# Banded attention: GpSimd adds each key tile's weights in one operation of 1024 columns instead of two of 512

## What is computed

```python
WINDOW = 128
s_ctx = jnp.einsum('bnqhgd,bchd->bnhgqc', qb, kc).astype(jnp.float32) * GQA_SCALE
s_band = jnp.einsum('bnqhgd,bnkhd->bnhgqk', qb, kb).astype(jnp.float32) * GQA_SCALE
valid = (jnp.abs(qpos - kpos) <= WINDOW) & (kpos >= 0) & (kpos < n)
s_band = jnp.where(valid[None, :, None, None], s_band, -jnp.inf)
p = jax.nn.softmax(jnp.concatenate([s_ctx, s_band, s_sink], axis=-1), axis=-1).astype(v.dtype)
o = (jnp.einsum('bnhgqc,bchd->bnqhgd', p[..., :nc], vc)
     + jnp.einsum('bnhgqk,bnkhd->bnqhgd', p[..., nc:nc + 3 * BLOCK], vb))
```

## Time and profile before

| | |
|---|---|
| median of 3 runs | 2767.04 us (2765.52 to 2770.16) |
| profiled execution: time, span | 2770.5 us, 2768.7 us |
| PE busy | 2566.3 us, 93% |
| PEld busy | 1979.2 us, 71% |
| DVE busy | 1419.2 us, 51% |
| ACT busy | 1153.6 us, 42% |
| POOL busy | 381.1 us, 14% |

### The profile page before, as it was taken

One profiled execution on the slowest core, in us unless ns is written; L12 is line 12 of the kernel. 1 busy time (PEld: TensorE's weight loads), 2 busy tenths in 40 slices (PEclk: granted clock), 3 DMA queues, 4 the chain that ended last, 5 costly groups with the idle time before them and its releaser, 6 DMA issues. The chain is left out here.

```text
span 2768.7 us, 38552 instructions
## 1 busy us (share of the span) xinstructions
PE 2566.3 (93%) x14759; PEld 1979.2 (71%) x14759; DVE 1419.2 (51%) x2283; ACT 1153.6 (42%) x1977; POOL 381.1 (14%) x415
## 2 busy tenths in 40 slices
PE   4999998999999999989999999899998999999787
PEld 3778987877778878933337778786334877798776
DVE  5113265666655514666764723411777547265752
ACT  6112344454454321134443622311767647333662
POOL 1000020010020000046761000000000010004710
PEclk8999999999999999989999999999999999998889
DMA  7430010000112131110002220102000220111012
GB/s 257 174 139 24 18 33 1 1 1 1 62 54 91 47 61 46 32 37 1 1 1 91 92 78 30 59 3 76 1 1 24 84 88 31 38 47 62 1 54 76
DMA packets 87991, 139.73 MB, mean 50 GB/s; under 512 B 19513, under 2 KB 54738, under 8 KB 87682
## 3 DMA queue, kind: packets, MB, share of 16 engines
q1 hardware_dynamic: 70592, 75.90, 8.8%
q0 software_dynamic: 16976, 61.30, 6.2%
q10 hardware_dynamic: 242, 0.07, 0.0%
HBM read 120.47 MB, written 16.78 MB: 50 GB/s over the span
## 5 line engine op out<-in xcount | busy, mean ns | idle before, releaser
L169 ACT ACTIVATE WORK<-PS 128x512 f32<-128x512 f32 (+5 forms) x309 | 152.6, 494 | 659.2 <-PE PS L863 388.7
L863 PE MATMUL PS<-HT_R,W_R 128*128 128x512 f32 (+1 forms) x896 | 334.3, 373 | 0.0
L862 PE MATMUL PS<-WORK_R,W_R 128*128 128x512 f32 (+1 forms) x736 | 271.4, 369 | 0.0
L861 PE MATMUL PS<-WORK_R,W_R 128*128 128x512 f32 (+1 forms) x672 | 250.0, 372 | 14.4 <-DVE W_R L169 9.9
L169 ACT ACTIVATE HT<-PS 128x1024 f32<-128x1024 f32 (+6 forms) x211 | 156.0, 739 | 161.0 <-PE PS L1296 126.4
L989 PE MATMUL PS<-WORK_R,HT_R 128*128 128x512 f32 x528 | 210.3, 398 | 8.8 <-DVE W_R L169 7.5
L863 PE MATMUL PS<-W_R,WORK_R 128*128 128x256 f32 (+3 forms) x704 | 215.2, 306 | 0.0
L990 PE MATMUL PS<-WORK_R,MIXT_R 128*128 128x512 f32 x544 | 214.1, 394 | 0.0
L991 PE MATMUL PS<-W_R,HT_R 128*128 128x512 f32 x528 | 207.4, 393 | 0.0
L862 PE MATMUL PS<-W_R,HT_R 128*128 128x256 f32 (+2 forms) x688 | 206.2, 300 | 0.0
L926 PE MATMUL PS<-BASE,WORK 128*128 128x128 f32 (+1 forms) x1186 | 175.2, 283 | 25.3 <-DVE WORK L169 16.8
(11 more groups left out here) (328 smaller groups left out, 5587.3 us busy)
## 6 DMA issues: line engine op xcount, KB each, us to landing
MIXT<-in_w_mod POOLq DMA_DIRECT2D x8, 2048.0 KB, 8.7
x_scratch<-WORK POOLq DMA_DIRECT2D x24, 512.0 KB, 2.9
WORK<-x_scratch POOLq DMA_DIRECT2D x24, 512.0 KB, 3.6
W<-in_odd_w_in SPq DMA_DIRECT2D x12, 1024.0 KB, 5.2
W<-in_even_w_in SPq DMA_DIRECT2D x5, 2048.0 KB, 7.9
W<-in_w_mod SPq DMA_DIRECT2D x4, 2048.0 KB, 20.8
WORK<-in_x POOLq DMA_DIRECT2D x16, 512.0 KB, 8.7
W<-in_e_w_in SPq DMA_DIRECT2D x6, 1024.0 KB, 5.9
```

The source lines that it names most:

```text
L169: self.last = Signalled(self, issue(*args, **kwargs))
L861: mm(out, a[0], b_[0], start=k == 0, stop=False)
L862: mm(out, a[1], b_[0], start=False, stop=False)
L863: return mm(out, a[0], b_[1], start=False, stop=k == KT - 1)
```

## The change

The loop over the two halves goes; one operation adds all 1024 columns of a step. The buffers, the waits around a step and the step's one increment of `summed` stay. There are 60 such sums (76 steps less the 16 with k = 0), so that 120 operations become 60. No other engine's instructions change, neither in number nor in order.

```diff
@@ -3261,10 +3261,7 @@
                         if k == 1 and m >= 2:
                             pool.wait_ge(totalled, m - 1)
                         total = psum_of(m)
-                        was = halves8(GPT[(n - 1) % 3]) if k == 1 else total
-                        for par in range(2):
-                            added = add_up(total[:, par, :], was[:, par, :], halves8(GPT[n % 3])[:, par, :], ALU.add)
-                        added.then_inc(summed, 1)
+                        add_up(total, halves8(GPT[(n - 1) % 3]) if k == 1 else total, halves8(GPT[n % 3]), ALU.add).then_inc(summed, 1)
                         if k == 2 and done < 2 * KT and m >= 4:
```

## The result

The changed kernel takes 2782.02 us (median of 6 runs, 2777.11 to 2783.96); the kernel before, run beside it, 2768.48 (6 runs, 2765.52 to 2774.22). The ratio is 1.0044, with an interval of 1.003 to 1.0058: slower, by less than half a per cent. The profiled execution took 2778.17 us with a span of 2776.3, which is 7.6 more than the span of before.

What follows compares the result with a forecast made beforehand. PE bounds the kernel, through its waits for DVE, which POOL's operations hold. Terms 6.5 + 0.9 + 2.8 - 0.7 + 2.9 = 12.4 us take the profiled execution from 2770.5 to 2782.9; median 3.5 below, so 2779.5, range 2773.5 to 2785.

Steps and rivals of the forecast that it cites:

- PE's four waits of two groups: Ahead of PE's fifth top (L1324) and transpose (L1348), odd and even groups; DVE ends each; 1.93 us more in all.
- The merged sum: POOL's sum of 1024 columns takes 2.37 us, bounds 2.30 and 2.45, instead of 2.62 for a pair.
- The odd group's fifth top: At L1324, the whole sum holds DVE's low parts, so PE starts 1.09 us later.
- Its transpose: Odd group's transpose (L1348): DVE waits for a whole sum, but the last 8 columns find POOL idle; adds 0.
- The even group: Low parts ahead of the fifth top +0.13 us; SCALAR_TENSOR_TENSOR ahead of the transpose waits for a whole sum, +0.71.
- The stage: Banded attention: odd fifth tops 6.5, even ones 0.9, even transposes 2.8, first groups -0.7, end +2.9; sum 12.4 us.
- the term there: Group 13 and the last two groups: operations such as the diagonal's wait for a whole sum, estimated +2.9 us in all.
- The clock: Rival, 7%: longer PE waits in the last groups bring one or two more lower-clock stretches, 2 to 5 us more.
- ended inside a sum: Rival, 7%: the 1024-column sum lets DVE in halfway, say at 1.2 us; -4.5 us, 2762.5.
- the tie at the SCALAR_TENSOR_TENSOR: At both transposes POOL's sum comes 0.10 us first; rival, 7%: DVE passes first, +5.5 us, 2772 to 2773.
- 24 places in twelve groups: Range: four places per two groups follow the sum's length one to one; 2.30 takes 1.7 us off, 2.45 adds 1.9.
- The hold: A DVE operation with inputs in SBUF and a POOL operation exclude each other; whoever comes first keeps the place.

Runs made afterwards that it cites:

- The two part kernels: Against the kernel before, only each group's first sum (k = 1) merged, or only the others (k > 1), the rest kept as halves: 1.0036 and 1.0016.
- The fill kernel: Against the changed kernel, POOL fills the 1024 columns with 1.0 instead of each merged sum, reading nothing; softmax's denominator left out: 2750.7 us, one run.
- shorter pieces: Each sum as four operations of 256 columns instead of one of 1024, in the old order: 0.9982 against the kernel before.
- quarters: Sums as four operations of 256 columns, first sum behind the low parts, slab subtractions behind a group's last sum: 0.9948 against the kernel before.
- halves and merged sums with both moves: First sum waits for the low parts, slab subtractions move from k = 2 to k = 4; two 512-column sums or one of 1024: 0.9976 and 0.9964 against before.

## Why the prediction was right

*The place.* PE's four waits of two groups set the stage's pace. The 33.2 to 33.3 us that remain in all twelve rows of the table bear this out.

*The merged sum.* 2.37 us taken from the 1280-column row; 58 of the 60 take 2.34 to 2.40, the other two were held themselves.

*The odd group's fifth top.* Forecast +1.09, measured +1.11 (gap 0.11 to 1.22). Its low parts take 2.25 us where I had said 2.2.

*Its transpose.* Forecast 0, measured -0.05. The reason given was right as well: a whole sum held the SCALAR_TENSOR_TENSOR, and the last 8 columns found POOL idle (0.17). The two part kernels show that the zero belongs to both parts together: each alone shortens this wait, by 0.88 and 0.54.

*The even group.* Forecast +0.13 and +0.71, measured +0.13 and +0.67. Two groups: +1.85, forecast +1.93.

*The stage.* From the first fifth top to the last, +9.4 us, where the terms gave 6.5 + 0.9 + 2.8 - 0.7 = 9.5. Ahead of the first nothing changed (-0.1). Behind the last fifth top it is +4.3, and the term there was +2.9. PE's waits there grew by 2.8 (0.68 at the transpose of group 13, 0.10 at the top of 1432.12, 1.10 ahead of the L1373 of 1449.97 and 0.95 at the transpose of 1455.61), so the term was right as a sum, though its parts, "1.09 each, with some slack", weren't worked out one by one. **The other 1.5 us are the clock, which the sum had at nothing.** In all +13.65 instead of +12.4.

*The clock.* It was one rival, at 2 to 5 us for one or two stretches more at the lower level. No stretch was added, but the one behind the stage's last long wait became 6.8 us long instead of 3.4, for 1.5 us. The other rivals fell: none of DVE's two-input operations ended inside a sum; the tie at the SCALAR_TENSOR_TENSOR went to POOL by 0.10 to 0.13 us; the waits reached PE.

*What was wrong in the working.* "24 places in twelve groups" that follow the sum's length is too many. By the prediction's own terms an odd group's transpose adds 0 whatever the length, so 17 places do (6 + 7 + 4): the bounds are then 1.2 down and 1.4 up, not 1.7 and 1.9, a sum of 2.25 us would take 2 us off the total and not 3, and a hold would have to be given up earlier than after 1.9 us to eat the 12.4. The hold was also put too widely, as one of any DVE operation with its inputs in SBUF. A one-input reduce in SBUF isn't held: in after the one below runs while POOL's second slab subtraction does (from 1360.08 to 1361.36). This changes no term of the sum.

```profile
1360.23 0.18 DVE L169 TENSOR_REDUCE SMX<-HT 128x8 f32<-128x24 f32 x1
```

*The measurement.* 2782.0 against 2779.5 forecast. 1.25 of the 2.5 us are the stage, and the rest is that the kernel before gave 2768.5 beside it, not 2767.0.

The SBUF — State Buffer page of the Trainium skill (Who interferes with whom) says that a GpSimd operation that only writes doesn't contend with a two-input DVE one, but that an operation such as tensor_scalar can enter a mode that takes the shared port pair and then contends with any. The fill kernel's trace agrees with both: 0.69 us, and 0.87 us in the one case.

## What to carry to other kernels

When two engines exclude each other for whole instructions, an instruction's length is a cost to the other engine, and merging two saves its own engine's time only: in the timeline, find operations whose duration doesn't fit their size, and see whose end they share. Then look at which engine the bound engine waits for; here shorter pieces were faster (0.9982) with 22% more work on POOL than the merged sums, and best was to put POOL's sums and slab subtractions where DVE has no two-input work (0.9948 with quarters). Count both sides of such a move: a wait taken away at one place came back at the next until the work behind it was moved too. And read a total with its clock: stretches at the lower level made up 1.5 of the 13.65 us of the change, and 5.7 of the 7.8 us between halves and merged sums with both moves.

## What the runs showed of the hardware

- A one-input TENSOR_SCALAR of 8 columns, read from SBUF and written to it, was held by a POOL operation that reads nothing, to 0.87 us (one case); two-input TENSOR_TENSORs weren't (13 cases, 0.42 to 0.43 us for 256 columns and 0.69 for 512).
- A one-input TENSOR_REDUCE of 24 columns in SBUF took its 0.18 us in the middle of a POOL operation that reads SBUF.
- POOL's cost is nearly linear: sums took 0.73 us for 256 columns, 1.27 for 512 and 2.37 for 1024, about 0.18 us fixed and 2.13 ns a column; the fill took 0.95 us for 1024.
